# PSUM operands for VectorE in the retrieval, and the fetched u rows dealt 96, 24 and 8 to retrieval, gates and experts

## The reference, cut to what matters

```
def peer(h, w_q, sub_keys, u_tab, v_tab):
    q = (h @ w_q).reshape(B, T, PEER_HEADS, 2, PEER_HALF)          # 8 heads, two halves of 128
    s = jnp.einsum('bthpd,hpnd->bthpn', q, sub_keys)               # scores against 2 x 128 sub-keys
    v1, i1 = lax.top_k(s[..., 0, :], K)                            # K = 16
    v2, i2 = lax.top_k(s[..., 1, :], K)
    cand = (v1[..., :, None] + v2[..., None, :]).reshape(..., K * K)
    cidx = (i1[..., :, None] * PEER_NKEYS + i2[..., None, :]).reshape(..., K * K)
    top_s, pos = lax.top_k(cand, K)
    eidx = jnp.take_along_axis(cidx, pos, axis=-1)                 # 8 x 16 = 128 experts of 16384 per position
    gates = jax.nn.softmax(top_s, axis=-1)
    ...
        u = jnp.take(u_tab, ib, axis=0)
        act = jax.nn.gelu(jnp.einsum('btd,bted->bte', hb, u), approximate=False)
        vv = jnp.take(v_tab, ib, axis=0)
        return jnp.einsum('bte,bted->btd', gb * act, vv)
```

## Time and profile before

| | |
|---|---|
| median of three runs | 2096.85 us |
| profiled execution, its span | 2092.45 us, 2090.2 us |
| busy TensorE / VectorE / ScalarE / GpSimd | 1850.1 / 1503.6 / 726.9 / 813.8 us |
| retrieval, dense heads (PE's first piece behind the row ring to its last) | 826 to 1130 us |
| gates | 1136 to 1440 us, then some 12 us until TensorE's first expert product |
| experts | 1452 to 2078 us, then 12 us to the end |

### The profile page before, as it was taken

The page is one execution under the profiler, slowest core; times in us unless marked ns, Lnnn a source line. Parts: engine busy times, 40 slices in busy tenths (PEclk is TensorE's granted clock), DMA queues, the critical chain, the costliest instruction groups (busy, mean ns, idle before and its releaser), DMA issues. The chain is left out here.

```text
span 2090.2 us, 32362 instructions
## 1 busy us (share of the span) xinstructions
PE 1850.1 (89%) x11429; PEld 1622.5 (78%) x11429; DVE 1503.6 (72%) x2853; ACT 726.9 (35%) x1073; POOL 813.8 (39%) x451
## 2 busy tenths in 40 slices
PE   2998868878998897999998988976999999999997
PEld 1775557776876687989897988976999888888886
DVE  5999554443332477999998888876778788777776
ACT  3335322223323423333333344423333333333333
POOL 1444211113442245889785222221345444333330
PEclk8999867778999899999999999988999999999999
DMA  8661000002221224888785787887888999988883
GB/s 314 243 209 50 11 2 1 0 0 81 100 91 50 101 91 159 262 259 264 252 269 196 232 270 249 266 289 221 294 286 316 342 371 367 343 324 318 319 325 130
DMA packets 178050, 431.98 MB, mean 207 GB/s; under 512 B 15160, under 2 KB 91064, under 8 KB 177856
## 3 DMA queue, kind: packets, MB, share of 16 engines
q1 hardware_dynamic: 125568, 274.36, 38.1%
q0 software_dynamic: 36864, 134.23, 18.7%
q10 hardware_dynamic: 15552, 22.55, 2.9%
HBM read 383.38 MB, written 47.71 MB: 206 GB/s over the span
## 5 line engine op out<-in xcount | busy, mean ns | idle before, releaser
L182 POOL DMA_INDIRECT own_rows<-in_peer_v_dram,own_row x128 | 215.3, 1682 | 327.8 <-DVE y_own L1853 309.1
L182 POOL DMA_INDIRECT own_rows<-in_u_rows_dram,own_row x128 | 193.3, 1510 | 306.4 <-DVE own_rows L1581 233.4
L1763 PE MATMUL bank<-v_hi,coef_lo 128*128 128x512 f32 x768 | 299.2, 390 | 0.0
L1763 PE MATMUL bank<-v_lo,coef_hi 128*128 128x512 f32 x768 | 299.2, 390 | 0.0
L1763 PE MATMUL bank<-v_hi,coef_hi 128*128 128x512 f32 x768 | 298.8, 389 | 0.1
L1233 PE MATMUL bank<-h_hi,piece_hi 128*128 128x384 f32 (+1 forms) x672 | 241.4, 359 | 28.7 <-POOL piece_lo L1370 25.6
L1370 POOL TENSOR_TENSOR piece_lo<-piece,piece_hi 128x1024 fp32r<-128x1024 f32 x84 | 211.8, 2522 | 128.8 <-ACT piece_hi L1300 128.0
L1233 PE MATMUL bank<-h_lo,piece_hi 128*128 128x384 f32 (+1 forms) x672 | 236.4, 352 | 0.0
L1233 PE MATMUL bank<-h_hi,piece_lo 128*128 128x384 f32 (+1 forms) x672 | 236.3, 352 | 0.0
L1300 ACT ACTIVATE piece_hi<-piece 128x1024 fp32r<-128x1024 f32 x84 | 89.1, 1060 | 284.2 <-PE bank L1233 208.0
L1838 DVE TENSOR_TENSOR v_lo<-v_tile,v_hi 128x1024 fp32r<-128x1024 f32 x128 | 156.5, 1223 | 24.5 <-ACT v_hi L1794 22.4
(11 more groups left out here) (341 smaller groups left out, 4134.1 us busy)
## 6 DMA issues: line engine op xcount, KB each, us to landing
v_tile<-in_peer_v_dram SPq DMA_DIRECT2D x128, 512.0 KB, 5.2
piece<-in_peer_u_dram SPq DMA_DIRECT2D x68, 512.0 KB, 4.3
ada<-in_w_ada_dram SPq DMA_DIRECT2D x48, 512.0 KB, 5.0
gate_scratch<-gate_block SPq DMA_DIRECT2D x12, 2048.0 KB, 11.5
gate_tiles<-gate_scratch SPq DMA_DIRECT2D x32, 768.0 KB, 7.0
gelu_scratch<-gelu_early ACTq DMA_DIRECT2D x104, 192.0 KB, 4.0
gelu<-gelu_scratch SPq DMA_DIRECT2D x104, 192.0 KB, 5.5
u_early<-in_peer_u_dram SPq DMA_DIRECT2D x36, 512.0 KB, 7.4
```

Source lines behind the costliest of these rows:

```text
L182: pool.indirect_dma_start(own_rows[:, n % R], None, tables[n // NS], bass.IndirectOffsetOnAxis(ap=own_row[:, n % NS:n % NS + 1], axis=0)). ...
L1763: last = nc.tensor.matmul(y_bank(t, half)[:], w[:, j, t * P:(t + 1) * P], x[:, j, c], start=(first and n == 0), stop=(final and n == 2))
```

## The change

Four things, all in the retrieval, and one constant:

1. Operands in PSUM. `h_psum` is a pair of adjacent banks (6 and 7) that holds the own tile's h. The dots in the retrieval read it there instead of its SBUF copy `h_own`; the copy is still made, and the dots of the gates and experts still read it. In bank 4 lie `fi`, `abf`, `ab` and `ab_eq`, in bank 5 `score`: the small tiles of top-k that VectorE writes and reads.
2. So that no instruction reads two PSUM tiles, some tiles of the index arithmetic go to SBUF (`ab_in`), "mask" becomes pos - 8a, which waits for "shift", and the head's largest score is first copied to SBUF ("gmax") in the two softmaxes.
3. Early pieces accumulate in banks 0 and 1 instead of 4 and 5; the three transposes at the stage's end go to banks 2, 3 and 4.
4. DOT_HEAD is 12 and DOT_ITER 4 (were 8 and 8): 96 u rows are used in the retrieval, at the places `fill(0)` to `fill(7)` as 1, 2, 1, 2, 1, 2, 1, 2; 24 in the gates, at units 1, 3, 5 and 7 of each iteration; 8 in the experts, one in each of the first eight steps. GpSimd's fetches follow: 1 and 2 in turn ahead of the pieces of a head.

```diff
-DOT_HEAD, DOT_ITER = 8, 8
+DOT_HEAD, DOT_ITER = 12, 4
...
     if p < OWN_GELU:
-        return 2
+        return 1
...
-        bank = [top.enter_context(nc.psum_tensor(f"bank{i}", [P, 512], F32)) for i in range(8)]
+        bank = [top.enter_context(nc.psum_tensor(f"bank{i}", [P, 512], F32)) for i in range(6)]
+        bank_pair = top.enter_context(nc.psum_tensor("bank_pair", [P, D], F32))
+        bank += [bank_pair[:, 512 * n:512 * n + 512] for n in range(2)]
...
+    h_psum = g_["bank_pair"]
+    look = bank[4][:].rearrange("p (x n t k) -> p x n t k", x=4, n=2, t=TT)
+    fi, abf, ab, ab_eq = look[:, 0], look[:, 1], look[:, 2, 0].bitcast(U32), look[:, 2, 1]
+    score = bank[5][:].rearrange("p (t h k) -> p t h k", t=TT, h=PH)
...
                     if e >= 2:
                         pe.wait_ge(gelu_done, e - 1)
-                    product(n, bank[4 + e % 2][:, 0:TD], TD)
+                    else:
+                        pe.wait_ge(q_ready, NQ - 1 + e)
+                    product(n, bank[e % 2][:, 0:TD], TD)
...
-                    a_, r_, e9, e1, i_, j_ = ab[:, 0, S], ab[:, 1, S], ab_eq[:, 0, S], ab_eq[:, 1, S], abf[:, 0, S], abf[:, 1, S]
+                    a_, e9, i_, j_ = ab[:, S], ab_eq[:, S], abf[:, 0, S], abf[:, 1, S]
+                    r_, e1, i0 = (ab_in[:, n, S] for n in range(3))
                     nc.vector.tensor_scalar(a_, pos[:, S], 3, None, ALU.logical_shift_right).then_inc(*V.step("shift"))
-                    nc.vector.tensor_scalar(r_, pos[:, S], 7, None, ALU.bitwise_and).then_inc(*V.step("mask"))
+                    dve.wait_ge(*at("shift"))
+                    nc.vector.scalar_tensor_tensor(r_, a_, -8.0, pos[:, S], ALU.mult, ALU.add).then_inc(*V.step("mask"))
...
-                    nc.vector.tensor_tensor(th(g), th(sc), th(sc)[:, :, 0:1].to_broadcast([P, n, TOPK]), ALU.subtract).then_inc(*V.step("gsub"))
+                    top = gsum[:, 1, t0:t1].rearrange("p t h -> p (t h)")
+                    nc.vector.tensor_copy(top, th(sc)[:, :, 0]).then_inc(*V.step("gmax"))
+                    dve.wait_ge(*V.after("gmax"))
+                    nc.vector.tensor_tensor(th(g), th(sc), top.unsqueeze(2).to_broadcast([P, n, TOPK]), ALU.subtract).then_inc(*V.step("gsub"))
...
-                        nc.vector.scalar_tensor_tensor(rows[:, i % R], rows[:, i % R], 1.0, h_own[:], ALU.mult, ALU.mult,
+                        nc.vector.scalar_tensor_tensor(rows[:, i % R], rows[:, i % R], 1.0, h_psum[:], ALU.mult, ALU.mult,
                                                        accum_out=own_act[:, bass.ds(n, 1)]).then_inc(row_used, 1)
 
-                    topk(VB, h, DENSE, dot)
+                    def dots(at):
+                        for i in range(at * DOT_HEAD // 8, (at + 1) * DOT_HEAD // 8):
+                            dot(i)
+
+                    topk(VB, h, DENSE, dots)
...
-                nc.vector.tensor_copy(gateT[:, 0:TD], bank[2][:, 0:TD]).then_inc(*VP.step("gT"))
+                nc.vector.tensor_copy(gateT[:, 0:TD], bank[4][:, 0:TD]).then_inc(*VP.step("gT"))
```

More of the change, by code:

```diff
@@ L1165, in retrieve_stage @@
         iu = sb(ctx, "top_half_at", [P, 2, TT, TOPK], U32)
-        fi = sb(ctx, "top_half_key", [P, 2, TT, TOPK])
         cand = sb(ctx, "candidates", [P, TT, KC])
@@ L1169, in retrieve_stage @@
         pos = sb(ctx, "top_at", [P, TT, TOPK], U32)
-        ab = sb(ctx, "top_ab", [P, 2, TT, TOPK], U32)
-        ab_eq = sb(ctx, "top_ab_eq", [P, 2, TT, TOPK])
-        abf = sb(ctx, "top_ab_f", [P, 2, TT, TOPK])
+        ab_in = sb(ctx, "top_ab_in", [P, 3, TT, TOPK])
         hot = sb(ctx, "rank_hot", [P, 2, TT, K2])
-        score = sb(ctx, "top_all", [P, TT, PH, TOPK])
         sel = sb(ctx, "key_all", [P, 2, TT, PH, TOPK])
@@ L1189, in steps @@
             n += ["key", "cand_a", "cand_b", "cand_c"] + [f"{x}{t}" for x in ("cmax", "cat", "crest", "cmax2_", "cat2_") for t in ts_]
-            return n + ["score", "shift", "mask", "row9", "row1", "i_row", "j_rest", "i_all", "j_all", "hot0", "hot1", "pick0", "pick1", "sel0", "sel1"]
+            return n + ["score", "shift", "mask", "row1", "i_row", "row9", "j_rest", "i_all", "j_all", "hot0", "hot1", "pick0", "pick1", "sel0", "sel1"]
         pre_v = ["scale_p", "scale2"] + [f"xn{t}" for t in range(TT)] + [f"lo{k}" for k in range(KT)]
-        own_v = ["gsub", "own_f", "own_row", "gsum", "grec", "own_gate", "h_own"]
-        post_v = ["gsub", "gsum", "grec", "gates", "idx0", "idx1", "gT"]
+        own_v = ["gmax", "gsub", "own_f", "own_row", "gsum", "grec", "own_gate", "h_own"]
+        post_v = ["gmax", "gsub", "gsum", "grec", "gates", "idx0", "idx1", "gT"]
         sv = sem(ctx, "rt_vector")
@@ L1291, in _ @@
                         src = (sel[:, n, t] if n < 2 else gates[:, t]).rearrange("p h k -> p (h k)")
-                        last = nc.tensor.transpose(bank[n][:, t * P:(t + 1) * P], src, C["ident"])
+                        last = nc.tensor.transpose(bank[2 + n][:, t * P:(t + 1) * P], src, C["ident"])
                     last.then_inc(turned, 1)
@@ L1309, in early @@
                         act.wait_ge(stored[e % 2], 16 * (e // 2))
-                    nc.scalar.activation(gel[:, e % 2, :], bank[4 + e % 2][:, 0:TD], ACT.Gelu).then_inc(gelu_done, 1)
+                    nc.scalar.activation(gel[:, e % 2, :], bank[e % 2][:, 0:TD], ACT.Gelu).then_inc(gelu_done, 1)
                     act.wait_ge(gelu_done, e + 1)
@@ L1504, in _ @@
                 for n in range(2):
-                    last = nc.vector.tensor_copy(h_own[:, 512 * n:512 * n + 512], bank[6 + n][:])
+                    last = nc.vector.tensor_copy(h_own[:, 512 * n:512 * n + 512], h_psum[:, 512 * n:512 * n + 512])
                 last.then_inc(*VO.step("h_own"))
@@ L1522, in _ @@
                     dve.wait_ge(turned, n + 1)
-                    nc.vector.tensor_copy(idxT[:, n, 0:TD], bank[n][:, 0:TD]).then_inc(*VP.step(f"idx{n}"))
+                    nc.vector.tensor_copy(idxT[:, n, 0:TD], bank[2 + n][:, 0:TD]).then_inc(*VP.step(f"idx{n}"))
                 dve.wait_ge(turned, 3)
-                nc.vector.tensor_copy(gateT[:, 0:TD], bank[2][:, 0:TD]).then_inc(*VP.step("gT"))
+                nc.vector.tensor_copy(gateT[:, 0:TD], bank[4][:, 0:TD]).then_inc(*VP.step("gT"))
 def scatter_stage(nc, a, env, spill, acts):
```

7 lines of the change are left out of this document (3 added, 4 removed).

## The result

| | before | after |
|---|---|---|
| median (range) of 20 runs each | 2093.52 us (2083.05 to 2106.16) | 2108.06 us (2085.39 to 2114.44) |
| ratio, 95% interval | | 1.0054 (1.0035 to 1.0073) |
| profiled execution, its span | 2092.45, 2090.2 us | 2111.05, 2108.8 us |

Forecast was 2066 us, faster. The profiled executions differ by 18.6 us, somewhat more than the medians (14.5). The difference lies in two stages. The last split of the retrieval starts at 1133.4 us instead of 1123.1, 10.3 us later. The first low half of a gates piece is then made at 1151.1 us and the last at 1449.7, 298.5 us apart where it was 290.3, 8.2 us more. From there the distance stays what it was. Of the 10.3 us some 7 lie between the eight dense heads (by the first reduction of ranks, 38.2 us a head before and 39.2 after); the rest stands before the first and behind the last.

The account below looks back on a forecast made before the run. VectorE and GpSimd were taken to lock each other out in the retrieval, and transfer plus VectorE to set the gates. Gains of 13 us (retrieval), 18 (gates) and 0 (experts) sum to 31: 2096.85 - 31 = 2066 us, range 2038 to 2091.

Parts of the forecast that it names:

- What bounds the kernel: VectorE and GpSimd lock each other out in the retrieval; the gates' loop is 14.5 us of transfer and 9.8 of VectorE.
- Part 1: Retrieval: operands in PSUM save VectorE 10.7 us a head, from 38.6 to 27.9 us.
- rivals C and D: C: fetches stay long, GpSimd bounds the retrieval, 2115 us, chance 0.05. D: PSUM dots are held all the same, 2135, 0.03.
- Part 2: Retrieval: with 32 more dots a head takes 37 us, 1.6 less than now, 13 us gained in all.
- The load loop: Retrieval: split, landing, rounding and split of pieces take 32 us a head, 34.8 if landing takes 5.0 us.
- the ring: Retrieval: the ring of four row slots for fetches is the longest loop, 36.9 us a head.
- rival B: More bytes lengthen both landings in the retrieval, heads 38 us or more; gain 7 us, 2090; chance 0.14.
- Rival A: The ring doesn't bind, TensorE sets the retrieval, gates near TensorE's 21.7 us a half; gain 56 us, 2041; chance 0.25.
- Part 3: Gates: 24 fewer dots save 1.5 us of each 24.3 us half iteration, 18 us in all.
- Floor: 11 halves x 1.14 = 12.5 us: Gates: least gain, from taking one 1.14 us dot out of VectorE's 9.8 us in each half's loop.
- Nothing here gets longer: Gates: no step lengthens with fewer dots; the ring has more room, with half the dots.
- Part 4: Experts: eight fewer dots change nothing, 0 us, since TensorE is the bound there.

Follow-up runs that it names:

- deal_only: The kernel before with the new deal of rows (DOT_HEAD 12, DOT_ITER 4), all operands in SBUF: 2166.42 us, ratio 1.0358 to the kernel before.
- psum_only: The kernel after with the old deal of rows (DOT_HEAD 8, DOT_ITER 8), operands in PSUM: 2074.31 us, ratio 0.990 to the kernel before.
- ring6: The kernel after with six row slots for the fetches instead of four: 2090.04 us, ratio 0.9987 to the kernel before.
- piece3: The kernel after with a third landing buffer for the retrieval's pieces: 2103.97 us, ratio 1.0026 to the kernel before.
- ring6_piece3: The kernel after with six row slots and three landing buffers for pieces: 2072.94 us, ratio 0.9891 to the kernel before.
- filler: The kernel after with 12 unused matmuls added in each of units 2 and 6 of the gates: 2086.95 us, ratio 0.9961 to the kernel before.
- load_first: The kernel after with the gates' next piece sent ahead of the 2 MB write: 2050.15 us, ratio 0.9793 to the kernel before.

## Why the prediction was wrong, step by step

**What bounds the kernel.** The reading of VectorE and GpSimd locking each other out held. That the gates have a loop through the load and the write held too. The reading closed it through VectorE's 9.8 us, where the table above closes it through TensorE's product and the next write, and it missed that the loop's length also depends on TensorE's clock, which stood in rows 1 as 0.92 and was not used.

**Part 1, right.** Dots 1212 ns (forecast 1220), ranks 949 and 944 (945), no second mode; fetches 0.956 us (0.96): rivals C and D did not occur. The Trainium skill's inference against it (SBUF — State Buffer, "Who interferes with whom") would have left the fetches at the 1.77 us of rows 8; every one of 76 fetches took 0.93 to 1.04 us once the dots read PSUM, and with SBUF operands in the same deal their median is 1.46. The fetches that lie beside a dot took 1.76 us at the median in the kernel before and in deal_only (45 and 54 of them), 0.96 in the kernel after (35). The measurement decides against the inference. The one price that was left open, a PSUM write, came out as 261 ns instead of 210 for the cast of 96 elements, 50 ns, inside its bounds. Alone this part gives 19 us (psum_only).

**Part 2, failed: 39.2 us a head, not 37.** Two terms of the step "what is late next" were mis-sized, and treated as separate. The load loop was given 32 us, 34.8 with a landing of 5.0. Landing did rise, from 4.3 at the median to 4.9, and its maximum from 6.4 to 8.6:

```profile
DMA to landing us min/median/max: 3.2/4.9/8.6
```

The mean went from 4.40 to 5.29 us. For four loads a head in each of the two buffers this adds 3.6 us, and a split stands in GpSimd's order behind one or two fetches, each of which may wait for a slot, which the 32 left out (the size of this second part is argued, not measured). ring6, where slots no longer hold GpSimd (0.3 us), still has 37.6 us a head: the load loop is that long. piece3, where pieces no longer hold ScalarE, has 38.8: the ring is that long, against 36.9 worked out. Which of the ring's terms was too small wasn't measured; its five pieces at 4.19 us assume that TensorE never waits, and it waited. In the kernel after the head is 39.2; that the two loops delay each other's transfers and GpSimd's stream is argued from this. What was called rival B (both landings lengthen, 38 us or more), at a chance of 0.14, is what happened here, though the rows' landing hardly grew (median 6.2 to 6.4 us) and the pieces' did. It cost 23 us against the forecast, 10.3 more instead of 13 less, 18 of them by 8 x (39.2 - 37). Rival A's head (34.8 us, TensorE the bound) is nearly reached by ring6_piece3, with both loops opened.

**Part 3, failed: 26.5 us a half on most of the way, not 22.8.** Two steps failed. The first is the "Floor: 11 halves x 1.14 = 12.5 us". It takes the dot out of a loop that runs through VectorE's 9.8 us. But the load can't leave ahead of the write before it in the queue, and that write follows TensorE's product, 3.6 us behind its last matmul in both kernels. So one dot less brought the loads nearer to their writes by 4.5 us in all (23.6 to 19.2). The second, and the larger, is "Nothing here gets longer". The time saved joined TensorE's idle stretch in front of the piece that lands late, and the matmuls behind it ran at half the clock: 119 slow steps instead of 58, which made the products 12.2 us longer. The loads took 1.3 us more, where the forecast had given them up to 1.5 us a half less. From write to write this makes 8.8 us, and the stage grew by 8.2.

The 18 us exist: deal_only's profiled gates took 271.9 us. But there 9.7 of them come from loads that land sooner, 4.4 from products with fewer slow steps and only 4.0 from the shorter way to the load, so that even this agreement in size is in part luck. Part 3 cost 26 us against the forecast, somewhat more than part 2. No rival contained it.

**Part 4, right.** The experts take 626 to 627 us with 16, 8 or 40 dots.

**Sum.** -13 - 18 us was forecast. It was +10.3 up to the end of the retrieval and +8.2 in the gates, 18.5 of the 18.6 us between the profiled executions.

**Open.** What puts a run into one or the other course of the gates. Of deal_only and the kernel after, both start with an early fetch and a late load (12.9 and 12.8 us), and only deal_only leaves that course in the next half. Both courses occur in one execution: ring6's profiled halves are 26.5 and 26.1 us near the start, then 22.8, 23.6, 21.3 and 22.9. The kernel after spreads over 29 us in 20 runs, and its one profile lies at the long end, so that this spread is the two courses is argued, not shown. Open too is a part of the way from deal_only's and filler's halves of 22.2 and 22.5 us, with the old order and the clock at 0.96 and 0.97, to load_first's 19.4. deal_only's products behind a write mostly have 0.7 to 2.1 us of idle time ahead of them and load_first's none, which leaves over 1 us a half unexplained.

## What to carry to other kernels

Before handing an in-order chain more transfers, walk round every loop that shares its buffers (here row ring and load loop) and relax both in thought. Here they were worked out as 36.9 and 32 to 34.8 us; opening one alone gave 1.6 or 0.4 us a head, both together 3.7. When you put an instruction into a loop, ask what the transfer behind it waits for besides: here the write ahead of it in the queue, which another engine released. Taking work off an engine that isn't the bound can make a stage slower, if it gathers the bottleneck's idle time into fewer, longer stretches: look at the matmuls' step behind each pause, and at the granted clock of the stage, before costing a saving. And ask of every small load what large write stands ahead of it in its queue; moving a load ahead of each write gained 34 to 58 us, where the operands in PSUM gained 19.

## What the runs showed of the hardware

- A load of 512 KB sent right behind a 2 MB write of the same queue could be used 13.3 us after its sending in the half shown, and 10.7 or 12.6 us after it at the mean, by whether a row fetch was sent 4.9 us or more, or less, behind the write. With a load ahead of each write the stage's wait for pieces halved and the program was 34 to 58 us shorter.
- VectorE instructions with two SBUF inputs lengthen GpSimd's indirect fetches, not only its arithmetic: median 1.46 us in deal_only, 0.956 with one operand in PSUM, same deal; beside a dot 1.76 and 0.96.
- Adding 144 unused matmuls, or 24 unused VectorE instructions of 1.2 us, to a stage of 298 us shortened it by 21 to 22 us.
- ring6_piece3 moved 340 GB/s over 200 us, with DMA share 0.96, and TensorE was busy 198 of them: the 306 GB/s of the kernel after were not a limit of the memory.
